# An expert loop of two quads and three passes in place of four quads and one pass, and wide dummy products on TensorE in the last quad

## What is computed

```python
def hier_moe(h, w_grp, b_grp, w_exp, b_exp, w_gate, w_up, w_down):
    # top 1 of 4 groups, then top 2 of the 8 experts of that group
    ...
    for g in range(N_GROUPS):
        hid = (jax.nn.silu(jnp.einsum('nd,edf->nef', hf, w_gate[g]))
               * jnp.einsum('nd,edf->nef', hf, w_up[g]) * combine[:, g, :, None])
        out = out + jnp.einsum('nef,efd->nd', hid, w_down[g])
```

## Time and profile before

| what | value |
| --- | --- |
| median of 3 runs | 450.44 us (449.57 to 452.26) |
| the profiled execution, its own time | 450.19 us |
| its span (first to last record) | 448.1 us |
| mean granted TensorE clock over the span | 0.97 of full |
| PE busy | 409.2 us, 91% |
| DVE, ACT, POOL busy | 189.1, 156.1, 38.9 us |
| device memory read, written | 138.06 MB, 1.05 MB |

### The profile page before, as it was taken

The page is one execution under the profiler, slowest core; times in us unless marked ns, Lnnn a source line. Parts: engine busy times, 40 slices in busy tenths (PEclk is TensorE's granted clock), DMA queues, the critical chain, the costliest instruction groups (busy, mean ns, idle before and its releaser), DMA issues.

```text
span 448.1 us, 8018 instructions
## 1 busy us (share of the span) xinstructions
PE 409.2 (91%) x3286; PEld 310.5 (69%) x3286; DVE 189.1 (42%) x352; ACT 156.1 (35%) x303; POOL 38.9 (9%) x80
## 2 busy tenths in 40 slices
PE   7999999999999999999999989989869848978964
PEld 6999999899999999999898634434333413633621
DVE  3674766776558956645555312221211202111103
ACT  5734564656439535475727210000000000001003
POOL 4010232323100000000400200000000000000000
PEclk9999999999999999999999999999988959989988
DMA  7978875667774687655999999999999999999983
GB/s 234 295 204 270 263 240 181 218 225 217 244 256 133 202 282 264 194 185 166 352 359 369 375 423 420 419 423 419 422 422 420 421 421 419 423 418 408 410 306 140
DMA packets 56233, 139.62 MB, mean 312 GB/s; under 512 B 5350, under 2 KB 39174, under 8 KB 46982
## 3 DMA queue, kind: packets, MB, share of 16 engines
q1 hardware_dynamic: 55840, 138.31, 82.9%
q10 hardware_dynamic: 358, 0.80, 0.5%
HBM read 138.06 MB, written 1.05 MB: 310 GB/s over the span
## 4 chain that ended last, share of the span: by engine, by line
PE 72%; DMA 18%; SPq 5%; ACT 2%; issue 1%; DVE 1%; POOLq 0%; POOL 0%; DVEq 0%; ACTq 0%
PE proj L1291 13%; PE proj L1292 13%; PE proj L1293 13%; DMA moe_pair<-in_expert_w_up_dram 12%; PE proj L1578 7%; PE score L1601 5%; SPq L379 4%; DMA moe_pair<-in_expert_w_down_dram 4%; PE score L1533 3%; PE proj L1559 2%; PE attno L1371 1%; PE attno L1635 1%; PE probt L1293 1%; PE probt L1292 1%; PE probt L1291 1%
## 5 line engine op out<-in xcount | busy, mean ns | idle before, releaser
L872 DVE TENSOR_TENSOR w_lo<-w_raw,w_hi 128x1024 fp32r<-128x1024 f32 x64 | 78.6, 1231 | 40.8 <-ACT w_hi L622 40.4
L622 ACT ACTIVATE w_hi<-w_raw 128x1024 fp32r<-128x1024 f32 x64 | 67.6, 1058 | 36.7 <-PE proj L1293 20.1
L1291 PE MATMUL proj<-hT_hi,w_hi 128*128 128x256 f32 x232 | 67.5, 291 | 1.8 <-DVE hT_lo L863 1.4
L1292 PE MATMUL proj<-hT_lo,w_hi 128*128 128x256 f32 x232 | 65.6, 283 | 0.0
L1293 PE MATMUL proj<-hT_hi,w_lo 128*128 128x256 f32 x232 | 65.6, 283 | 0.0
L1578 PE MATMUL proj<-moe_pair,moe_x 128*32 128x512 f32 x384 | 50.1, 669 | 14.9 <-DMA moe_pair<-in_expert_w_up_dram 14.9
L1211 DVE TENSOR_TENSOR moe_x<-score,gains_moe 128x256 f32<-128x256 f32 x32 | 13.6, 425 | 92.3 <-PE score L1533 92.3
L815 ACT ACTIVATE hid<-proj 128x256 f32<-128x256 f32 x8 | 3.1, 384 | 137.3 <-PE proj L1578 113.9
L1291 PEld LDWEIGHTS proj<-hT_hi,w_hi 128*128 128x128 f32 x232 | 44.3, 191 | 5.5 <-issue 3.6
L1292 PEld LDWEIGHTS proj<-hT_lo,w_hi 128*128 128x128 f32 x232 | 44.4, 191 | 0.0
L1293 PEld LDWEIGHTS proj<-hT_hi,w_lo 128*128 128x128 f32 x232 | 44.4, 191 | 0.0
(11 more groups left out here) (281 smaller groups left out, 782.3 us busy)
## 6 DMA issues: line engine op xcount, KB each, us to landing
moe_pair<-in_expert_w_down_dram SPq DMA_DIRECT2D x26, 1024.0 KB, 26.1
moe_pair<-in_expert_w_gate_dram SPq DMA_DIRECT2D x24, 1024.0 KB, 18.9
moe_pair<-in_expert_w_up_dram SPq DMA_DIRECT2D x24, 1024.0 KB, 20.8
w_raw<-in_w_in_dram SPq DMA_DIRECT2D x33, 512.0 KB, 4.6
moe_pair<-in_expert_w_gate_dram SPq DMA_DIRECT2D x16, 512.0 KB, 11.0
moe_pair<-in_expert_w_up_dram SPq DMA_DIRECT2D x16, 512.0 KB, 11.4
moe_pair<-in_expert_w_down_dram SPq DMA_DIRECT2D x12, 512.0 KB, 6.8
w_raw<-in_xattn_wkv_dram SPq DMA_DIRECT2D x8, 512.0 KB, 3.9
```

What stands on the lines that cost most here:

```text
L622: act.activation(w_hi[g % NS][:], w_raw[:, g % NW], ACT.Copy).then_inc(hi_done, 1)
L872: dve.tensor_tensor(w_lo[g % NS][:], w_raw[:, g % NW], w_hi[g % NS][:].bitcast(F32), ALU.subtract)\
L1291: pe.matmul(ps, a[0], b[0], start=start, stop=False, skip_group_check=True)
L1292: pe.matmul(ps, a[0], b[1], start=False, stop=False, skip_group_check=True)
```

## The change

The loop's body becomes two quads. Quad 0 is written out, the loop takes quads 1 and 2, 3 and 4, 5 and 6 in three passes, quad 7 stands behind it. On SP quads 1 and 2 are written out (chunks 12 to 35) and two passes load quads 3 and 4, then 5 and 6. `trips` holds the passes less one, in pairs of quads (2 for one round). PE reads it in its first quad, between the gate and up products and the transposes. The 14 dummies ahead of quad 6 go. In the last quad four dummies of 512 columns take the place of the four of 128 (by the same name of bank, SC[0]), and four more of 512 columns are added after the transposes of the hidden rows, ahead of the down products. The order of transfers, the slots and who waits for whom are otherwise as before.

```diff
@@ constants
-    WARM_LOOP, WARM_LAST = 14, 4
+    WARM_UP, WARM_DOWN = 4, 4
-    BODY_QUADS = 4
-    BODIES, BODY_CHUNKS = QUADS // BODY_QUADS, BODY_QUADS * MOE_CHUNKS
+    PAIR_CHUNKS = 2 * MOE_CHUNKS
+    ROUND_PAIRS = QUADS // 2
     SLOTS = 24
-    LAST_QUAD = BODY_QUADS - 1
+    LAST_QUAD = 1
@@ SP
-            LAST = LAST_QUAD * MOE_CHUNKS
-            for i in range(SLOTS, LAST):
+            for i in range(SLOTS, SLOTS + MOE_CHUNKS):
                 sp.wait_ge(chunk_used, user_before(i))
-                load_whole(i, 0)
+                load_whole(i, 2)
...
-            with sp.Fori(0, turns) as turn:
-                for i in range(LAST, LAST + BODY_CHUNKS):
-                    sp.wait_ge(chunk_used, turn * BODY_CHUNKS + user_before(i))
-                    load_whole(i % BODY_CHUNKS, (turn + i // BODY_CHUNKS) % BODIES)
+            with sp.Fori(0, more) as turn:
+                for i in range(SLOTS + MOE_CHUNKS, SLOTS + MOE_CHUNKS + PAIR_CHUNKS):
+                    sp.wait_ge(chunk_used, turn * PAIR_CHUNKS + user_before(i))
+                    load_whole(i, (turn * 2 + i // MOE_CHUNKS) % QUADS)
@@ ACT
-            for q in range(LAST_QUAD):
-                expert_quad(q)
+            expert_quad(0)
...
-            with act.Fori(0, turns) as turn:
-                for q in range(LAST_QUAD, LAST_QUAD + BODY_QUADS):
-                    expert_quad(turn * BODY_QUADS + q)
+            with act.Fori(0, more + 1) as turn:
+                expert_quad(turn * 2 + 1)
+                expert_quad(turn * 2 + 2)
@@ DVE
-            dve.tensor_scalar(trips[:], nover[:], float(BODIES), float(BODIES - 1), ALU.mult, ALU.add).then_inc(trips_set, 1)
+            dve.tensor_scalar(trips[:], nover[:], float(ROUND_PAIRS), float(ROUND_PAIRS - 2), ALU.mult, ALU.add).then_inc(trips_set, 1)
...
-            for q in range(LAST_QUAD):
-                expert_quad(q, experts_of(q), experts_of(q + 1))
+            expert_quad(0, experts_of(0), experts_of(1))
             dve.wait_ge(trips_set, 1)
...
-            with dve.Fori(0, turns) as turn:
-                body, next_body = turn % BODIES, (turn + 1) % BODIES
-                expert_quad(turn * BODY_QUADS + LAST_QUAD, experts_of(LAST_QUAD, body), experts_of(0, next_body))
-                for q in range(LAST_QUAD):
-                    expert_quad(turn * BODY_QUADS + (BODY_QUADS + q), experts_of(q, next_body),
-                                experts_of(q + 1, next_body))
+            with dve.Fori(0, more + 1) as turn:
+                quads = [(turn * 2 + i) % QUADS for i in range(1, 4)]
+                for i in range(2):
+                    expert_quad(turn * 2 + i + 1, experts_of(quads[i]), experts_of(quads[i + 1]))
@@ PE
+            def warm_wide(bank, times):
+
+                for _ in range(times):
+                    pe.matmul(bank[:].rearrange("p (n q) -> p n q", n=4), ident[:],
+                              ident[:].unsqueeze(1).broadcast_to([P, 4, P]), start=True, stop=True)
@@ gate_up_by_columns
                         if q == LAST_QUAD and kh and j:
-                            warm(SC[0], WARM_LAST)
+                            warm_wide(SC[0], WARM_UP)
@@ first_quad
                 gate_up_by_columns(0, 0, first_in, PJ[0][:, FE:2 * FE])
+                pe.wait_ge(trips_set, 1)
+                more = pe.value_load(trips[0:1, 0:1], min_val=ROUND_PAIRS - 2, max_val=ROUND_PAIRS * ROUNDS - 2)
                 transposes(0, hid_halves)
@@ last_quad
                 transposes(n, hid_halves)
+                warm_wide(PJ[0], WARM_DOWN)
                 pe.wait_ge(hidT_sb, n + 1)
@@ the end of PE's program
-            first_quad()
-            for q in range(1, LAST_QUAD):
-                whole_quad(q, q, 0)
-            pe.wait_ge(trips_set, 1)
-            turns = pe.value_load(trips[0:1, 0:1], min_val=BODIES - 1, max_val=BODIES * ROUNDS - 1)
-            with pe.Fori(0, turns) as turn:
-                whole_quad(LAST_QUAD, turn * BODY_QUADS + LAST_QUAD, turn)
-                for q in range(LAST_QUAD):
-                    if q == LAST_QUAD - 1:
-                        warm(PJ[0], WARM_LOOP)
-                    whole_quad(q, turn * BODY_QUADS + (BODY_QUADS + q), turn + 1)
-            last_quad(turns * BODY_QUADS + LAST_QUAD)
+            more = first_quad()
+            with pe.Fori(0, more + 1) as turn:
+                whole_quad(1, turn * 2 + 1, turn * 16 + 16)
+                whole_quad(0, turn * 2 + 2, turn * 16 + 16)
+            last_quad(more * 2 + 3)
```

More of the change, by code:

```diff
@@ L104, in hybrid_layer @@
     GU_CHUNKS, MOE_CHUNKS = KD, KD + KF * 2
-    BODY_QUADS = 4
-    BODIES, BODY_CHUNKS = QUADS // BODY_QUADS, BODY_QUADS * MOE_CHUNKS
+    PAIR_CHUNKS = 2 * MOE_CHUNKS
+    ROUND_PAIRS = QUADS // 2
     SLOTS = 24
-    LAST_QUAD = BODY_QUADS - 1
+    LAST_QUAD = 1
     def slot_of_chunk(i):
         return i % SLOTS
-    def landed(i, body):
-        q = i // MOE_CHUNKS
-        return body * 32 + (0, 16, 16, 32)[q]
     def user_before(i):
@@ L368, in load_half, with load_whole @@
                 sp.dma_start(w_raw[:, g % NW], halves[g]).then_inc(w_in_sem[g % NW], 16)
-            def load_whole(i, body):
-                q, c = divmod(i, MOE_CHUNKS)
-                s, e0 = slot_of_chunk(i), (body * BODY_QUADS + q) * QE
+            def load_whole(i, quad):
+                s, c, e0 = slot_of_chunk(i), i % MOE_CHUNKS, quad * QE
                 if c < GU_CHUNKS:
@@ L399, in load_first @@
                 if i >= MOE_CHUNKS:
-                    load_whole(i, 0)
+                    load_whole(i, 1)
                 elif i < GU_CHUNKS:
@@ L472, in _ @@
             load_first(23)
[L473 to L474 removed]
+            for i in range(SLOTS, SLOTS + MOE_CHUNKS):
                 sp.wait_ge(chunk_used, user_before(i))
[L476 removed]
+                load_whole(i, 2)
             sp.wait_ge(trips_set, 1)
[L479 to L483 removed]
+            more = sp.value_load(trips[0:1, 0:1], min_val=ROUND_PAIRS - 2, max_val=ROUND_PAIRS * ROUNDS - 2)
+            with sp.Fori(0, more) as turn:
+                for i in range(SLOTS + MOE_CHUNKS, SLOTS + MOE_CHUNKS + PAIR_CHUNKS):
+                    sp.wait_ge(chunk_used, turn * PAIR_CHUNKS + user_before(i))
+                    load_whole(i, (turn * 2 + i // MOE_CHUNKS) % QUADS)
             for c in range(MOE_CHUNKS):
[L485 removed]
+                sp.wait_ge(chunk_used, more * PAIR_CHUNKS + user_before(3 * MOE_CHUNKS + c))
                 load_last(c)
@@ L819, in expert_quad @@
                 act.activation(y0_sb[:], SC[0][:], ACT.Copy).then_inc(y_act, 1)
-            for q in range(LAST_QUAD):
-                expert_quad(q)
+            expert_quad(0)
             act.wait_ge(trips_set, 1)
-            turns = act.value_load(trips[0:1, 0:1], min_val=BODIES - 1, max_val=BODIES * ROUNDS - 1)
-            with act.Fori(0, turns) as turn:
-                for q in range(LAST_QUAD, LAST_QUAD + BODY_QUADS):
-                    expert_quad(turn * BODY_QUADS + q)
-            expert_quad(turns * BODY_QUADS + LAST_QUAD, GU_CHUNKS - 2)
+            more = act.value_load(trips[0:1, 0:1], min_val=ROUND_PAIRS - 2, max_val=ROUND_PAIRS * ROUNDS - 2)
+            with act.Fori(0, more + 1) as turn:
+                expert_quad(turn * 2 + 1)
+                expert_quad(turn * 2 + 2)
+            expert_quad(more * 2 + 3, GU_CHUNKS - 2)
             act.dma_start(fin_g[:], final_norm_g.rearrange("(a n) -> a n", a=1).broadcast_to([P, D])).then_inc(fin_in, 16)
@@ L832, in _ @@
                 for t in range(TT):
-                    act.wait_ge(back_ps[t][half], turns * BODY_QUADS + BODY_QUADS)
+                    act.wait_ge(back_ps[t][half], more * 2 + 4)
                     squares(FINAL_NORM, ACC[t][half][:], t, half, fin_rows)
@@ L1232, in expert_quad, with experts_of @@
                 dve.tensor_copy(y1_sb[:], SC[1][:]).then_inc(y_dve, 1)
-            def experts_of(q, body=0):
-                return bass.ds(body * (BODY_QUADS * QE) + q * QE, QE)
-            for q in range(LAST_QUAD):
-                expert_quad(q, experts_of(q), experts_of(q + 1))
+            def experts_of(quad):
+                return bass.ds(quad * QE, QE)
+            expert_quad(0, experts_of(0), experts_of(1))
             dve.wait_ge(trips_set, 1)
-            turns = dve.value_load(trips[0:1, 0:1], min_val=BODIES - 1, max_val=BODIES * ROUNDS - 1)
-            with dve.Fori(0, turns) as turn:
-                body, next_body = turn % BODIES, (turn + 1) % BODIES
-                expert_quad(turn * BODY_QUADS + LAST_QUAD, experts_of(LAST_QUAD, body), experts_of(0, next_body))
-                for q in range(LAST_QUAD):
-                    expert_quad(turn * BODY_QUADS + (BODY_QUADS + q), experts_of(q, next_body),
-                                experts_of(q + 1, next_body))
-            expert_quad(turns * BODY_QUADS + LAST_QUAD, experts_of(LAST_QUAD, BODIES - 1), up=LAST_UP)
```

(15 more changed lines are left out.)

## The result

The changed kernel takes 451.88 us (median of 19 runs), the kernel before 450.49 beside it (20 runs): ratio 1.003, interval 1.002 to 1.004. A twentieth run of the changed kernel was slow, 586.9 us at a mean granted clock of 0.66, and is left out. That is 0.3% slower, inside the 0.5% called no difference, 0.5 us above the forecast of 451.4. The profiled execution took 450.68 us with a span of 448.9. The total came out right, and so did the path that sets it. Two readings behind it did not: that the loop leaves the end of the weights' stream where it was, and that the clock in quad 6 is lost for want of the 14 dummies.

What follows compares the result with a forecast made beforehand. The prediction took the stream of weights and the tail behind it as the bound; 450.19 us plus 1.04 (quad 6's clock) and 0.21 (last quad), with 0 for the loop, gave 451.4 us, range 448.6 to 454.2.

Steps and rivals of the forecast that it cites:

- The bound: Experts' stage: the stream of weights, not PE, sets the time; after the last weights land, the tail sets the end.
- The reserve in quad 1: Quad 1, the thinnest place: PE may be 5.7 us late before the stream gets a hole.
- reading the trip count: PE's read of the trip count, moved into quad 0: taken as free, 0 us.
- The jumps: PE's two backward jumps: 0 to the end, since waits before quads 4 and 5 cover any fetches; uncovered, 2 to 8 us.
- rival 2: Loop's exit before quad 7: PE stands for one or two instruction fetches; 452 to 455 us, say 453.6; chance 0.18.
- the wait named in the prediction: PE's wait of 4.21 us before quad 4, taken to follow the first jump and cover its cost.
- The stream: Weights' stream: four or five fetches fewer if the body is kept, under 0.1 MB or 0.2 us; taken as 0.
- Rival 4: Weights' stream shortened by fewer fetches on one DMA engine that finished last; 448 us would take 3 us; chance 0.04.
- +1.04 us: Quad 6's first half without the 14 dummies: 6.14 us instead of 5.10 at a lower clock, making PE 1.04 us later.
- +0.21 us: Last quad: two longer sets of dummies just outweigh two waits and the clock regained, 0.21 us more.
- Rival 1: Last quad: dummies fit under the waits, so landings alone limit the tail at full clock; 449.2 us; chance 0.2.

Runs made afterwards that it cites:

- e1: The changed kernel with the four short dummies in the last quad as before, no wide ones: 448.11 us, ratio 0.995 against the kernel before.
- f1: The kernel before with the loop of pairs on PE alone and without the 14 dummies; short dummies in the last quad: 448.37 us, ratio 0.9963.
- f2: e1 with quads 1 and 2 written out and one pass of four quads on PE, other engines in pairs: 449.92 us, ratio 1.0001 against the kernel before.
- e2: The kernel before without the 14 dummies ahead of quad 6, nothing else: 450.43 us, ratio 1.0004.
- e3: The kernel before with the four plus four wide dummies in the last quad, keeping its loop and the 14 dummies: 452.09 us, ratio 1.0029.
- e4: The changed kernel with one wide dummy ahead of the last up products and two after the transposes: 448.17 us, ratio 0.9958 against the kernel before.
- g2: f1 with two PE passes, quads 5 and 6 written out, and 76 tiny dummy products in each wait before them: 450.24 us, ratio 1.0004 against the kernel before.
- f3: f1 with quads 1 and 2 written out on PE and two passes of the loop of pairs: 448.46 us, ratio 0.9972 against the kernel before.

## Why the prediction was right, and where its reasons were not

- **The bound** was read rightly: the stream of weights, full from 256 us on, and the tail behind it. The reserve in quad 1 held, the jumps' cost is hidden or nil, and nothing in the profile shows a cost of reading the trip count.
- **The jumps.** "I take 0" was right for what PE does: no gap at the start of a pass or at the exit but a wait for weights (rival 2 is out). The first jump, into quad 3, stands where PE has no wait to hide in (the wait named in the prediction is a quad later), and quad 3 follows quad 2 without a gap there. The reason I gave was a cover; the profile's is that nothing is fetched.
- **The stream.** This is the step whose reason failed: "four or five fetches fewer if the body is kept ... under 0.1 MB, or 0.2 us; I take 0". It spread a fetch evenly over 16 engines, where a transfer ends with its slowest. Measured: the stream ends 1.4 us sooner. The 0 still held in this kernel, for another reason: behind two sets of wide dummies PE is the last to be ready, and no weights are waited for. Where PE does wait for them the loop is worth -0.5% (e1), -0.4% (f1), some 2 us, of which the landings make about 1.4 (f2 against f1: 1.47, with the clock full in both) and the clock in the tail the rest. Rival 4 named the cause, one engine that finished last, got a chance of 0.04, and was priced at 3 us needed and nothing shown. The row that would have shown it was at hand: at the end of the stream before the change a single engine still moved weights, a share of 0.07 or one in sixteen (a window of the kernel before, columns as in the earlier trace rows):

```profile
436.15:436.45 0.30, 0.14 (x4) 0.00 (x0) 0.00 (x0) 0.10 (x1) 0.00 (x0) 1.00 0.07 27
```

- **The 14 dummies.** +1.04 us was read from three rows. e2 gives 1.0004, and the rows' difference is scatter. But the lateness itself is real: the half's usual 6.00 us is 0.9 above the row of 5.10 that the sum starts from, with the 14 or without. Short dummies leave a wait before the last up products that takes it up; the wide ones leave none. So the term belongs to the wide dummies, and it stood in the sum at about its size by luck of the row it was drawn from. In the changed kernel's profile it is 5.77 - 5.10 = 0.67.
- **The wide dummies.** +0.21 us. The steps of the working came out one by one. The two sets took 3.70 and 3.60 us where 3.44 was taken, 0.42 more together, which makes up for the 0.37 less of quad 6. On the old loop the wide dummies cost about 1.3 us (e3), as much as the forecast's 1.04 and 0.21 together.
- So the change is +1.3 us by the wide dummies and then nothing by the loop, and the forecast had +1.25 and 0. Taken in the other order, the loop gives -2 us and the wide dummies cost 3.2 to 3.6 on top (changed kernel against e4 and e1, by the ratios), since the landings they outlast then come earlier. That gain, which the change has and hides, is what the prediction missed. Rival 1's value (449.2), a tail at the landings' pace, is 1 us above that of e4, which has such a tail with the landings of the new loop.

## What to carry to other kernels

A stream of transfers over all DMA engines ends with the slowest of them, so work that takes one engine, such as fetching instructions, is to be counted per engine and not as a share of bytes; look at how far apart the engines end. In a stage that is bound by transfers a short loop can be worth having on an engine that has time to spare (here PE, f1), and instructions put into its idle time need not be free (g2). Whether it pays depends on the count: here 5 to 8 fetches cost the same, and 9 cost 1.4 us more. Dummies that keep a clock up must end before the landing they wait beside, with the landing of the new kernel, not of the old.

## What the runs showed of the hardware

- PE kept a body of two quads and ran it again without a fetch: none between 304.95 and 426.27 us in the changed kernel, where before five came in that time, and no gap on PE at the jumps but waits for weights. The rule of the Trainium skill quoted in the prediction ("Runtime: NRT & Kernel Launch", "Instruction fetch mechanics") speaks of a window of two pages of 16 KB. Before, those five fetches of 16 KB served four quads, so a pair is about 2.5 of them (an estimate) and the jump back reaches behind such a window; by the rule it should have fetched and stalled. The trace doesn't agree: PE held more than the two pages here. A jump to a block that it didn't hold is in no run.
- One fetch of 16 KB costs the engine it falls on 1.4 to 1.6 us of weights in mid-stream: its own 1.0 to 1.1, and a slower packet after it (774 to 856 ns for 8 KB, 441 for 4 KB, usually 313 and 160). Up to eight within a full stream cost a chunk no more than one; the ninth and tenth put one and two engines 1.5 us behind the others.
- The clock in the first half of a quad that starts after 4 to 8 us without work is low for a varying time: 4.93 (f3, quad 4) to 6.60 us (f1, quad 6) for the same 32 records, and 3.29 us of dummies before a wait of 3.6 to 3.9 us gave 5.10 and 6.51 us, within the same spread.
